# Feature-major projections of a two-block layer: each 512-column product followed by a 256-column product of the slab before

## The reference

```
proj = rmsnorm(x) @ w_in + b_in            # q, k, v, glu_a, glu_b, two gates
o_sb = stick_breaking_attention(q, k, v) @ w_sb_out
u    = silu(layernorm(conv31(glu_a * sigmoid(glu_b))))
y    = (sigmoid(gate_sb) * o_sb + sigmoid(gate_cv) * (u @ w_conv_out)) @ w_o
x    = x + rmsnorm(y)
x    = x + rmsnorm(square(relu(rmsnorm(x) @ w_up)) @ w_down)
# second block: a gated delta rule and an RWKV-7 scan side by side, their
# output through w_out, a cross attention to a memory, and a second
# feed-forward of the same shape (ffn_w1, ffn_w2); at the end an rmsnorm
```

## Time and profile before

| | |
|---|---|
| time, median of 3 runs | 2820.43 us (2819.78 to 2822.73) |
| profiled execution, span from first to last instruction | 2824.8 us |
| PE busy | 2775.9 us (98%) |
| PE weight loads busy | 2405.2 us (85%) |
| DVE busy | 1936.3 us (69%) |
| ACT busy | 1411.8 us (50%) |
| 512-column feature-major products (L514) | 5040 |
| 256-column feature-major products (L521) | 5164 in the records |

### The profile page before, as it was taken

One profiled execution on the slowest core, in us unless ns is written; L12 is line 12 of the kernel. 1 busy time (PEld: TensorE's weight loads), 2 busy tenths in 40 slices (PEclk: granted clock), 3 DMA queues, 4 the chain that ended last, 5 costly groups with the idle time before them and its releaser, 6 DMA issues.

```text
span 2824.8 us, 48248 instructions
## 1 busy us (share of the span) xinstructions
PE 2775.9 (98%) x18618; PEld 2405.2 (85%) x18618; DVE 1936.3 (69%) x2354; ACT 1411.8 (50%) x1807; POOL 116.7 (4%) x130
## 2 busy tenths in 40 slices
PE   9999999999999999999999999999999999999998
PEld 8888888888888888888887888788888888888886
DVE  7898887768646556465787676955877556565564
ACT  6545557566434444344666446544654344343444
POOL 0000000150000000000000000131200000000000
PEclk9999999999999999999999999999999999999999
DMA  7555545766566665666464444402546666666664
GB/s 244 184 180 177 172 157 165 234 188 199 187 194 189 191 193 186 195 190 191 140 208 138 131 121 121 141 4 77 186 157 192 193 190 190 192 189 192 189 191 151
DMA packets 415244, 487.92 MB, mean 173 GB/s; under 512 B 14960, under 2 KB 346736, under 8 KB 415072
## 3 DMA queue, kind: packets, MB, share of 16 engines
q1 hardware_dynamic: 413216, 478.55, 54.5%
q0 software_dynamic: 1856, 6.98, 0.7%
HBM read 482.33 MB, written 3.15 MB: 172 GB/s over the span
## 4 chain that ended last, share of the span: by engine, by line
PE 88%; DVE 6%; ACT 3%; issue 2%; DMA 1%; ACTq 0%; DVEq 0%; SPq 0%
PE pg L514 36%; PE pg L521 19%; PE pg L465 16%; PE pg L470 8%; DVE lo L370 2%; PE p L1214 1%; PE pg L476 1%; DVE work L924 1%; ACT hi L329 1%; PE p L1231 1%; PE p L1664 0%; DVE xa L782 0%; PE pg L1939 0%; DVE dnc L1331 0%; DVE work L902 0%
## 5 line engine op out<-in xcount | busy, mean ns | idle before, releaser
L370 DVE TENSOR_TENSOR lo<-raw,hi 128x1024 fp32r<-128x1024 f32 x895 | 1082.5, 1228 | 687.8 <-ACT hi L329 684.2
L329 ACT ACTIVATE hi<-raw 128x1024 fp32r<-128x1024 f32 (+1 forms) x894 | 935.6, 1056 | 1119.0 <-PE pg L521 658.3
L514 PE MATMUL pg<-xa,hi 128*128 128x512 f32 x4144 | 1049.1, 395 | 2.4 <-DVE work L417 1.1
L514 PEld LDWEIGHTS pg<-xa,hi 128*128 128x128 f32 x4144 | 746.5, 189 | 141.1 <-issue 1.8
L521 PEld LDWEIGHTS pg<-xa,lo 128*128 128x128 f32 x4208 | 572.9, 190 | 50.1 <-DVE lo L370 10.1
L521 PE MATMUL pg<-xa,lo 128*128 128x256 f32 x4208 | 588.2, 282 | 4.8 <-DVE lo L370 4.8
L465 PE MATMUL pg<-hi,xb 128*128 128x512 f32 x2048 | 506.0, 389 | 0.0
L465 PEld LDWEIGHTS pg<-hi,xb 128*128 128x128 f32 x2048 | 383.9, 188 | 79.4
L470 PE MATMUL pg<-lo,xb 128*128 128x512 f32 x1024 | 273.7, 389 | 0.0
L514 PE MATMUL pg<-xb,hi 128*128 128x512 f32 x896 | 226.9, 395 | 0.1
L470 PEld LDWEIGHTS pg<-lo,xb 128*128 128x128 f32 x1024 | 192.2, 188 | 39.9
(11 more groups left out here) (438 smaller groups left out, 1827.7 us busy)
## 6 DMA issues: line engine op xcount, KB each, us to landing
raw<-w_in SPq DMA_DIRECT2D x264, 512.0 KB, 4.4
raw<-ffn_w SPq DMA_DIRECT2D x256, 512.0 KB, 3.8
raw<-w_up SPq DMA_DIRECT2D x128, 512.0 KB, 3.7
raw<-w_down SPq DMA_DIRECT2D x128, 512.0 KB, 4.6
raw<-w_o SPq DMA_DIRECT2D x32, 512.0 KB, 4.6
raw<-w_out SPq DMA_DIRECT2D x32, 512.0 KB, 4.1
raw<-w_sb_out SPq DMA_DIRECT2D x16, 512.0 KB, 4.6
raw<-w_conv_out SPq DMA_DIRECT2D x16, 512.0 KB, 4.6
```

What stands on the lines that cost most here:

```text
L329: nc.scalar.activation(hi[:, slot, :, 0:g.tiles * P], raw[:, slot, :, 0:g.tiles * P], ACT.Copy).then_inc(hi_ready, 1)
L370: nc.vector.tensor_tensor(lo[:, slot, :, wide_], raw[:, slot, :, wide_], hi[:, slot, :, wide_].bitcast(F32), ALU.subtract).then_inc(lo_rea ...
L514: nc.tensor.matmul(pg[:, par, t, :], lhsT=hi[:, slot, k, c:c + P], rhs=g.x[:, kk, :], start=(j == 0 and k == 0), stop=False)
```

## The change

A new function, `lagged_pe`, issues PE's instructions in all feature-major projections but the `single` and `begun` ones. It works in steps. A step pairs the 512-column products of one slab with the 256-column products of the slab before it, product by product: hi, lo, hi, lo. Where a block has four slabs the pairing goes on across blocks, so that the last slab's lo products stand in the first step of the next block. Where a block has two slabs, it pairs within the block: hi alone, one paired step, lo alone. A projection's first step has hi products only, its last step lo products only. The waits for `hi_ready`, `lo_ready` and `evacuated` stand at the start of a step. `slab_used` is raised and `each` is called at the end of the step that holds the slab's lo products, and `after(v)` runs after the step that ends block v, which in four-slab blocks is the first of block v+1. The arithmetic, the slabs and the work of the other engines are as before.

```diff
+        def lagged_pe(pe, g, after, x_tiles, of, each):
+            across = g.groups >= RING
...
+            def step(now, earlier, waits=False):
+                if now:
+                    i, v, j = now
+                    if not j:
+                        pe.wait_ge(evacuated, g.b0 + i * g.unroll + v + 1)
+                    pe.wait_ge(hi_ready, g.slab(i, v, j)[2] + 1)
...
+                if earlier:
+                    pe.wait_ge(lo_ready, g.slab(*earlier)[2] + 1 + RING)
+                for t in range(g.tiles):
+                    for k in range(KG):
+                        if now:
+                            hi_product(*now, t, k)
+                        if earlier:
+                            ins = lo_product(*earlier, t, k)
+                if earlier:
+                    ins.then_inc(slab_used, 1)
+                    if each:
+                        each()
+            def block(i, v, waits=False, last=False):
+                if not across or isinstance(i, int) and not i and not v:
+                    step((i, v, 0), None, waits)
+                for j in range(1, g.groups):
+                    step((i, v, j), (i, v, j - 1), waits)
+                step(None if last or not across else (i, v + 1, 0), (i, v, g.groups - 1))
...
         def gemm_pe(pe, g, after=None, x_tiles=None, of=None, each=None, begun=0):
...
+            if not (g.tokens or g.single or begun):
+                lagged_pe(pe, g, after, x_tiles, of, each)
+                return
```

More of the change, by code:

```diff
@@ L477, in both_parts, with hi_product, lo_product @@
                                  rhs=g.x[:, kk, part * T:part * T + T], start=first and not part, stop=False)
+        def lagged_pe(pe, g, after, x_tiles, of, each):
+            across = g.groups >= RING
+            def hi_product(i, v, j, t, k):
+                par, slot = (g.b0 + v) % 2, g.slab(i, v, j)[0]
+                nc.tensor.matmul(pg[:, par, t, :], lhsT=hi[:, slot, k, t * P:(t + 1) * P], rhs=g.x[:, g.x_from + j * KG + k, :],
+                                 start=(j == 0 and k == 0), stop=False)
+            def lo_product(i, v, j, t, k):
+                par, slot = (g.b0 + v) % 2, g.slab(i, v, j)[0]
+                return nc.tensor.matmul(pg[:, par, t, 0:T], lhsT=lo[:, slot, k, t * P:(t + 1) * P],
+                                        rhs=g.x[:, g.x_from + j * KG + k, 0:T], start=False,
+                                        stop=(j == g.groups - 1 and k == KG - 1))
+            def step(now, earlier, waits=False):
[4 more added lines that the diff above has]
+                    pe.wait_ge(hi_ready, g.slab(i, v, j)[2] + 1)
+                    if waits and of:
+                        pe.wait_ge(evacuated, of.b0 + g.kg // 2 * (j + 1) + 2)
+                    elif waits:
+                        pe.wait_ge(x_ready, x_tiles + KG * (j + 1))
+                if earlier:
[16 more added lines that the diff above has]
+                step(None if last or not across else (i, v + 1, 0), (i, v, g.groups - 1))
+            n = g.blocks - 1
+            first = x_tiles is not None or bool(of) or across
+            head = min(g.unroll, n) if first else 0
+            for v in range(head):
+                block(0, v, waits=(x_tiles is not None or bool(of)) and not v)
+                if after:
+                    after(v)
+            if n > head:
+                run_blocks(pe, n - head, g.unroll, lambda i, v: block(i + head // g.unroll, v),
+                           (lambda t: after(t + head)) if after else None, each)
+            block(n // g.unroll, n % g.unroll, waits=(x_tiles is not None or bool(of)) and not n, last=True)
+            if after:
+                after(n)
```

## The result

The changed kernel takes **2854.9 us** (median of 4 runs, 2848.76 to 2857.20) against 2821.58 us for the kernel before on the same chip: a ratio of **1.0115, 95% interval 1.0101 to 1.0129**, so slower by 33 us. The forecast was 2812 us with a range of 2775 to 2850. The sign was wrong, and the time lies 4.9 us beyond the range's upper end.

The account below looks back on a forecast made before the run. PE was taken to bound the kernel through its product pace. From 2820.4 us, 11.1 came off for alternating pairs and 3 was added for side work, giving 2812 us, range 2775 to 2850.

Parts of the forecast that it names:

- What bounds the kernel: PE, busy 2775.9 of 2824.8 us, sets the end; its product pace decides, with about 49 us idle.
- The pace of an alternating pair: In paired steps, 349.1 ns a pair falls to 346.7, the steady sum; 4612 pairs gain 11.1 us; chance 0.38.
- the longest product of a run behind 256s is its second, not its first: In 512 runs, first takes 0.23 us, second 0.24; surplus needs a 512 after a 512, which alternation lacks.
- second reason: In a pair, the little the first 256 wins is about what the first 512 can lose, so both cancel.
- every 512 pays half a return: Rival for paired steps: half of a 16 ns return per 512, 354.7 ns a pair, 2849 us; chance 0.23.
- point of decision: Pair pace in paired steps from which the slower rival decides: 350.0 ns, 4 us, with side work 0.2%.
- Back-to-back issue gap: Skill rule for products: 325 ns a pair; as free weights' load rival, 111 us faster, 2712 us, chance 0.03.
- Slots come free later: nothing is won or lost: `slab_used` comes 1.84 us later; steady-stage margins shrink from 7.1 and 7.7 to 4.3 and 5.9 us, no stall.
- lo of a slab still comes right behind the hi products of the same slab: In gate projections PE's order keeps DVE's split deadline unmoved; existing waits of 1.8 us neither grow nor shrink.
- the distances stay: `each` shifts eight hi products for all steps; only core projections' ends lose cover, 0 to 9.2 us, 3 taken.
- one instance: End of `rl`, where PE waits 0.57 us for DVE; cover taken there is at most 1.84 us.
- The sum: Whole kernel: 2820.4 us less 11.1 for pace plus 3 for side work gives 2812 us.

Follow-up runs that it names:

- e8: Kernel before, in projections without side work, products reordered so a four-slab block has one return from 256 to 512 columns instead of four: 2818.39 us, ratio 0.9987.
- e4: Kernel before with odd slabs taking lo products first, then hi, so equal runs join to sixteen: 2824.75 us, ratio 1.0006.
- e3: Kernel before with hi and lo products of the same slab alternating, no lag, wait for `lo_ready` ahead of both: 2843.93 us, ratio 1.0078.
- e2: Changed kernel with two 512-column products, then two 256-column ones, instead of one and one: 2839.3 us, ratio 1.0063.
- e5: Changed kernel with runs of eight instead of alternation, and lo lagging a slab only inside a block, not across blocks: 2830.77 us, ratio 1.0029.
- e1: Changed kernel with eight hi products, then eight lo products in a step: the slabs' lag, also across blocks, without alternation: 2843.31 us, ratio 1.0071.
- e10: Kernel before with only the next block's wait for `evacuated` moved ahead of the last slab's lo products in four-slab projections with side work: 2829.01 us, ratio 1.0025.
- e12: Changed kernel with lo products 512 columns wide too, so more work; only the pace in `up1` is read: 3328.69 us, one time.

## Why the prediction was wrong, step by step

**What bounds the kernel: right.** PE's pace and its few waits decided, and the steady paces held (226.7 ns for a 512, 120 for a 256 in e8's and e4's long runs).

**The pace of an alternating pair: wrong for most pairs.** The forecast took 346.7 ns between 338.7 and 362.7; for five of six pairs of the changed kernel it is 353.3. The step that failed is the reason "the longest product of a run behind 256s is its second, not its first", from which it concluded that alternation has no surplus. In an alternation *every* 512 is a long one, 233 to 241 ns in `up1`. In a run of eight the second is indeed the longest, 236 ns by unrounded starts, but the first takes 233 and not 226.7, which the 0.23 us of the earlier trace rows could not tell. The forecast's second reason, that what a 256 wins cancels what a 512 loses, does hold where e3 runs at 346.7 ns: a 512 takes 4.8 more there and a 256 4.8 less. So the pace itself exists, but the prediction had no row that told when. The rival "every 512 pays half a return", 354.7 ns, was nearly right in price; its point of decision, 350.0 ns, is passed. Its time, 2849 us, was too low for the other reason, below.

Where the earlier trace rows showed runs of eight and of four, no row showed single products, and e2's 348.25 ns shows how little could be inferred: the same reasoning about returns would have put two-and-two above four-and-four. The Trainium skill, "TensorE: Matmul & The Clock Gate", section "Back-to-back issue gap", gives N/2.4 + 2.5 ns for an isolated warm product, an estimate of 325 ns for a pair. No run here comes near it; the shortest pace of alternating pairs is 346.7.

**"Slots come free later: nothing is won or lost": wrong.** In the steady stages it held. In `up1` of the changed kernel PE's hi products wait for nothing (the groups of instructions from 849 to 936 us):

```profile
L486 PE MATMUL pg<-xa,hi 128*128 128x512 f32 x228 | 79.6, 398 | 0.0
```

But `mv` pays 1.9 us. There DVE makes the next stage's tiles between its splits, so a split that starts later, because ACT's rounding waited for the slot, makes all that follows later. PE in e5, which has the lag alone:

```profile
666.12 2.11 PE L486 MATMUL pg<-xb,hi 128*128 128x512 f32 x8 [1.31 <-ACT hi L329]
```

The gate projections were said to be safe because "lo of a slab still comes right behind the hi products of the same slab". That is PE's order, but not the time in between. DVE's split (4.6 us for four) begins when the block before is done and DVE's chain behind it has run. Before, the next slab's eight hi products stood between that end and the wait for lo; now they are already spent. Before, in `gsb`:

```profile
257.74 0.39 PE L970 MATMUL p<-la,cst 128*128 128x128 f32 x2
257.88 2.10 PE L514 MATMUL pg<-xa,hi 128*128 128x512 f32 x8
...
259.82 1.19 PE L521 MATMUL pg<-xa,lo 128*128 128x256 f32 x8
```

With the lag, in e1:

```profile
260.72 0.39 PE L1035 MATMUL p<-la,cst 128*128 128x128 f32 x2
...
262.86 2.08 PE L486 MATMUL pg<-xa,hi 128*128 128x512 f32 x8 [1.76 <-DVE lo L370]
```

The wait of 1.76 us is the eight hi products (1.84 us) that were the cover. This reading rests on the trace alone: e10 and e5 show that it is neither the early wait nor the lag inside blocks, and no run moves the attention's step by itself.

**Side work, "the distances stay", 0 to 9.2 us, 3 taken: the term that was mis-sized.** Its one instance was sized right. At the end of `rl` PE waited 0.57 us before; the text said up to 1.84 more, and e5 shows 1.85 more (L1598 is L1533 of before):

```profile
1644.41 2.05 PE L1598 MATMUL p<-work 128*128 128x128 f32 x16 [2.42 <-DVE dn_n L1688]
```

The term failed in what it left out: something like it happens at a projection's start too. In `dn`, DVE waits for a PE step (L765) that `each` now calls behind eight more hi products, and these wait for the tiles that DVE makes next. e5:

```profile
1393.54 1.66 DVE L773 SCALAR_TENSOR_TENSOR resid<-p,vec,resid 128x256 f32<-128x256 f32 x4 [1.80 <-PE p L765]
```

Before, DVE did not wait there. And the largest piece was in no sentence of the prediction: a wait at the start of a step is passed *ahead* of the side work (e10, 7.1 us with an interval of 4.5 to 9.6). The prediction asked who would be late for the slots and did not ask it of `evacuated`.

**The sum.** 2820.4 - 11.1 + 3 became 2821.6 + 11.6 + 21.6. Either error alone would have turned the sign: with the pace as measured and 3 us for the rest the change loses 14.6 us, with the pace as forecast and the measured lag it loses 10.5. Of the 21.6 us of the lag, e10 accounts for 7, e5 for 8.6, if the two add; some 6 are read from the trace alone (by stage, e1 above e5: `gsb` 1.7, `glu` 1.8) or stay open. `rl` has 1.3 more in e1 as well, but there the granted clock was 0.91 from 1640 to 1660 us, where it was 1.00 in the `rl` of e5 and of the changed kernel, which lose the same 1.8. In the stages of the two cores the profiles of one kernel and the next differ by several us for another reason (last section), so that `rv` can't be divided more finely.

## What to carry to other kernels

Before moving products past a wait or a piece of side work, list for each engine what ran under them: products that moved ahead of a block's end no longer cover what that end sets off, and a wait placed at the head of a fused step stands in front of everything behind it. A loss of moved products was about the length of what moved (1.8 to 1.9 us each in `gsb`, `mv`, `dn` and `rl`, for 1.84 us of products), paid at every place where the chain was just in time; the moved wait in `rv` cost more; and a release moved behind a step that depends on it by way of another engine is paid on every turn of the circle. A pace that no row shows, such as products of two widths by turns, is best measured before a forecast rests on it, and in the surroundings it will have: here one order had two paces.

## What was not expected of the hardware

- 512 and 256 columns side by side: 353.3 or 346.7 ns for one-and-one, lasting until PE is interrupted, 348.25 for two-and-two, 350.6 for four-and-four, 349.1 for eight-and-eight, where the steady paces make 346.7. Two 512s by turns with other weights cost nothing (e12).
- A wait of 4 us can cost more than itself. In the changed kernel the windows around the wait in `rv` (us, busy time and count of PE, PEld, DVE, ACT and POOL, then the granted clock):

```profile
1820.00:1824.00 4.00, 2.96 (x16) 2.44 (x16) 3.97 (x4) 1.06 (x1) 0.00 (x0) 1.00 0.45 126
1824.00:1828.00 4.00, 0.05 (x1) 0.00 (x0) 3.93 (x5) 1.06 (x1) 0.00 (x0) 0.91 0.47 136
1828.00:1831.30 3.30, 3.28 (x10) 2.80 (x11) 3.23 (x5) 0.00 (x0) 0.00 (x0) 0.50 0.02 5
1831.30:1834.70 3.40, 3.40 (x13) 2.87 (x12) 1.84 (x3) 1.06 (x1) 0.00 (x0) 0.58 0.57 192
```

  Behind four us in which PE did nothing the clock was granted at half, 1.2 GHz, for some 7 us, and then rose again. In e10 it fell in the same place, and the core step there took about 5 us where it took 3.62. Over all of `rv` the granted clock was 0.96 in both, as before, and 1.00 in e8, whose profile is 4.6 us shorter in that stage though its order there is that of before: such falls lie at differing places from run to run, and single profiles of the core stages are uncertain by that much. The times go with it: the changed kernel took 2848.8 us at a mean granted clock of 0.997 and 2857.2 at 0.995, and the kernel before, in e1's comparison, 2820.4 to 2823.4 at 0.997. So, as an estimate from these times, some 5 of the 33 us go with the clock; whether the waits of the change bring them about, no run separates.
